# The first block of a two-block model on one core: the norm moved behind the projections, the state-space tables cut in four steps and interleaved with gate projections, memory and load order re-laid

## What is computed

```python
h = rms_norm(x, norm1_g[l])
p = h @ w_in[l]                                  # 1024 -> 512 u, 512 v, 256 s, 2 x 1024 gates
uv = jax.nn.gelu(p[..., :o_s5], approximate=False)
s_in = p[..., o_s5:o_gate]
gates = jax.nn.sigmoid(p[..., o_gate:] + b_gate[l])
br_a = gmlp_spatial_gating(uv[..., :GMLP_WIDTH], uv[..., GMLP_WIDTH:], ...)
br_b = s5_mixer(s_in, ...)                       # two complex linear recurrences, 16 groups of 64 states
merged = g_a * (br_a @ w_up_a[l]) + g_b * (br_b @ w_up_b[l])
x = x + merged @ w_out[l]
h2 = rms_norm(x, norm2_g[l])
x = x + expert_choice_ffn(h2, ...)               # 16 experts of 1024 x 2048 x 1024, 64 tokens each
```

## Time and profile before

| | us |
|---|---|
| median of 3 runs (lowest, highest) | 2056.41 (2055.82, 2056.73) |
| the profiled execution | 2056.92 |
| span of its instructions | 2055.1 |
| TensorE busy in the span | 1782.2 |
| VectorE, ScalarE busy | 675.9, 457.1 |
| start of chunk 19 on TensorE | 410.36 |
| first product of the experts done, ninth load issued | 478 |
| second block starts | about 1381 |

### The profile page before, as it was taken

One profiled execution on the slowest core, in us unless ns is written; L12 is line 12 of the kernel. 1 busy time (PEld: TensorE's weight loads), 2 busy tenths in 40 slices (PEclk: granted clock), 3 DMA queues, 4 the chain that ended last, 5 costly groups with the idle time before them and its releaser, 6 DMA issues. The chain is left out here.

```text
span 2055.1 us, 19088 instructions
## 1 busy us (share of the span) xinstructions
PE 1782.2 (87%) x7952; PEld 1063.1 (52%) x7952; DVE 675.9 (33%) x893; ACT 457.1 (22%) x571; POOL 0.2 (0%) x4
## 2 busy tenths in 40 slices
...
GB/s 140 1 23 136 41 87 72 181 224 272 428 428 428 428 429 428 429 429 429 429 429 429 429 429 428 428 424 166 2 162 43 101 63 102 103 82 110 94 62 41
DMA packets 75428, 492.45 MB, mean 240 GB/s; under 512 B 7024, under 2 KB 11632, under 8 KB 50544
## 3 DMA queue, kind: packets, MB, share of 16 engines
...
## 5 line engine op out<-in xcount | busy, mean ns | idle before, releaser
L670 PE MATMUL ps<-xs,xe 128*64 128x512 f32 x2048 | 461.5, 598 | 66.2 <-DMA xs<-w_up 34.7
L670 PEld LDWEIGHTS ps<-xs,xe 128*64 128x64 f32 x2048 | 141.7, 137 | 378.6 <-issue 264.6
L432 PE MATMUL ps<-xh,hi 128*128 128x512 f32 x576 | 231.8, 402 | 61.3 <-ACT hi L393 60.2
L402 DVE TENSOR_TENSOR lo<-raw,hi 128x2048 fp32r<-128x2048 f32 (+1 forms) x73 | 164.6, 2259 | 321.7 <-ACT hi L393 320.2
L682 PE MATMUL ps<-xs,hidT 128*64 128x512 f32 x1024 | 229.9, 596 | 14.7 <-DMA xs<-w_down 10.0
L432 PE MATMUL ps<-xl,hi 128*128 128x512 f32 x576 | 229.0, 398 | 0.0
L898 DVE TENSOR_TENSOR hid<-hid,ps 128x512 f32<-128x512 f32 x32 | 20.6, 684 | 524.6 <-PE ps L670 524.6
L393 ACT ACTIVATE hi<-raw 128x2048 fp32r<-128x2048 f32 (+1 forms) x73 | 137.5, 1891 | 204.4 <-PE ps L432 125.7
L432 PEld LDWEIGHTS ps<-xh,hi 128*128 128x128 f32 x576 | 111.5, 194 | 89.3 <-issue 61.6
L682 PEld LDWEIGHTS ps<-xs,hidT 128*64 128x64 f32 x1024 | 73.7, 136 | 149.2 <-issue 127.9
L432 PE MATMUL ps<-xh,lo 128*128 128x512 f32 x576 | 136.4, 389 | 0.0
(11 more groups left out here) (417 smaller groups left out, 1782.2 us busy)
## 6 DMA issues: line engine op xcount, KB each, us to landing
...
raw<-w_in SPq DMA_DIRECT2D x25, 1024.0 KB, 10.9
...
```

The source lines that it names most:

```text
L402: dve.tensor_tensor(lo[slot][:, 0:size], raw[:, n % NRAW, 0:size], hi[slot][:, 0:size].bitcast(F32), ALU.subtract).then_inc(sem("lo_done"), 1)
L432: mm = pe.matmul(ps[:, bank + m, 0:nn if token_major else SEQ], l, r, start=(k == 0 and part == 0 and q == 0), stop=(last and part == 1 an ...
L670: mm = pe.matmul(ps[64 * half:64 * half + 64, bank + b, :], xe[:, k, CAP * u:CAP * (u + 1)], xs[n % NXS][:, f:f + 512], start=(k == 0), st ...
```

## The change

The reading, by part:

- **Norm.** `xh` and `xl` are made from x times its gain alone, so chunk 0 needs no norm. The sums of squares move behind chunk 0. The reciprocal root `rb` is applied to the outputs: ACT scales s and v by token (`rtok`) as it empties PSUM, and for u and the gates DVE multiplies PSUM by `rb` into SBUF (`take`); the gelu and sigmoids of ACT then work in SBUF.
- **Order.** The table steps stand between chunks 2, 3, 4, 5 and 6; D after 6; gates a0, b0, a1 come ahead of u; Y and Z follow each other after chunk 10; a projection's second half follows its first at once, and the next waits for PSUM bank by bank (`taken_up_to`).
- **Tables.** `CL` has 9 instead of 17 lags and is kept for all groups, so the 16 copies `CO` go. The products with it write 32 rows each at four places of PSUM (`tables`); Y and Z write 64 rows at two.
- **Memory and loads.** The first block's ring has two slots; chunk n is loaded when chunk n-2 has been split. `INT` is filled by 32 copies instead of 8. Expert chunks 4, 5 and 1 are loaded before chunks 14 and 15.

```diff
-    for h in range(2):
-        first += group(w["w_in"], 1280 + 512 * h, 8) + group(w["w_in"], 2304 + 512 * h, 8)
+    first = group(w["w_in"], 1024, 8, 256) + group(w["w_in"], 512, 8)
+    for c in (1280, 2304, 1792, 0, 2816):
+        first += group(w["w_in"], c, 8)
...
-            if n >= NRAW:
+            if n >= NEXP + NRAW:
                 sp.wait_ge(sem("lo_done"), num(n, i, 1, 1 - NRAW))
-            sp.dma_start(raw[:, n % NRAW, 0:nk * nn].rearrange("p (k n) -> p k n", k=nk), src) \
-                .then_inc(sem(f"raw_in{n % NRAW}"), 16)
+            elif 2 <= n < NFIRST:
+                sp.wait_ge(sem("lo_done"), n - 1)
+            sp.dma_start(raw[:, raw_slot(n), 0:nk * nn].rearrange("p (k n) -> p k n", k=nk), src) \
+                .then_inc(sem(f"raw_in{raw_slot(n)}"), 16)
...
+            pe.wait_ge(sem("qq_taken"), first + 1)
+            return {(0, m): lambda m=m: pe.wait_ge(sem("qq_taken"), first + m + 2) for m in range(3)}
+
+        def first_pe(pe):
+
+            def tables(q):
+
+                pe.wait_ge(sem("tab_q"), q + 1)
+                pe.wait_ge(sem("s_tok"), NT)
+                if q:
+                    pe.wait_ge(sem("vt_done"), 2 * q)
+                for r in range(2):
+                    for g in range(GQ):
+                        mm = pe.transpose(ps[:, PP + r, g * P:(g + 1) * P],
+                                          V[q % 2][:, r, g].rearrange("p t h -> p (t h)"), ident)
+                mm.then_inc(sem("v_ps"), 1)
+                if q == 1:
+                    pe.wait_ge(sem("u_done"), 2)
+                if q >= 2:
+                    pe.wait_ge(sem("hs_done"), q - 1)
+                bank = PP + 2 + q % 2
+                for n, (c0, c1, side, lag) in enumerate(((0, 8, 1, 1), (8, 15, 0, 0), (7, 8, 0, 8))):
+                    for r in range(2):
+                        for j in range(4):
+                            g = GQ * q + j
+                            mm = pe.matmul(ps[32 * j:32 * j + 32, bank, c0 * SH:c1 * SH],
+                                           BF[side][:, r * SG + g:r * SG + g + 2, :].rearrange("p a h -> p (a h)"),
+                                           CL[:, r, g, lag:lag + c1 - c0, :].rearrange("p t h -> p (t h)"),
+                                           start=(n == 0 and r == 0), stop=(n == 2 and r == 1))
+                mm.then_inc(sem("h_ps"), 1)
...
+            norm_sums(pe, 0, QQ + 3)
+            chunk_mms(pe, 1, QQ, 0, 4, xh, xl, True, closes=False,
+                      after={(0, 2): lambda: pe.wait_ge(sem("nrm_rms"), 1)})
+            pe.wait_ge(sem("rb_done"), 1)
+            for t in range(NT):
+                mm = pe.matmul(ps[:, PP, SW + t:SW + t + 1], rb[:, t * P:(t + 1) * P], ident[:, 0:1], start=True, stop=True)
+            mm.then_inc(sem("rt_ps"), 1)
+            chunk_mms(pe, 2, QQ, 4, 4, xh, xl, True, opens=False)
+            tables(0)
+            chunk_mms(pe, 3, QQ, 0, 4, xh, xl, closes=False, after=taken_up_to(pe, 0))
+
...
+            tables(1)
+            chunk_mms(pe, 4, QQ, 4, 4, xh, xl, opens=False)
+            tables(2)
+            chunk_mms(pe, 5, QQ, 0, 4, xh, xl, closes=False, after=taken_up_to(pe, 4))
+            tables(3)
+            chunk_mms(pe, 6, QQ, 4, 4, xh, xl, opens=False)
+
...
+
+            chunk_mms(pe, 7, QQ, 0, 4, xh, xl, closes=False, after=taken_up_to(pe, 8))
+            chunk_mms(pe, 8, QQ, 4, 4, xh, xl, opens=False)
+            chunk_mms(pe, 9, QQ, 0, 4, xh, xl, closes=False, after=taken_up_to(pe, 12))
+            chunk_mms(pe, 10, QQ, 4, 4, xh, xl, opens=False)
+
+            pe.wait_ge(sem("ds_done"), 8)
+            pe.wait_ge(sem("sn_done"), 4)
+            pe.wait_ge(sem("int_in"), 16 * 4 * BL)
+            for g in range(SG // 2):
+                for c in range(2):
+                    o, gg = ps[64 * c:64 * c + 64, PP + g // 4, (g % 4) * P:(g % 4 + 1) * P], g + 8 * c
+                    pe.matmul(o, U[:, gg, :], INT[:, gg, :], start=True, stop=False)
+                    for r in range(2):
+                        mm = pe.matmul(o, Sn[:, r, gg, :], CL[:, r, gg, 0:8, :].rearrange("p t h -> p (t h)"),
+                                       start=False, stop=(r == 1))
+                if g % 4 == 3:
+                    mm.then_inc(sem("y_ps"), 1)
+
...
+            pe.wait_ge(sem("yblk_done"), 2)
+            for q in range(4):
+                for t in range(NT):
+                    for c in range(2):
+                        mm = pe.matmul(ps[64 * c:64 * c + 64, PP + q, t * P:(t + 1) * P],
+                                       vg[:, t, q * P + 64 * c:q * P + 64 * c + 64], wsT[:, 2 * q + c, :],
+                                       start=True, stop=True)
+                mm.then_inc(sem("z_ps"), 1)
+            chunk_mms(pe, 11, QQ, 0, 4, xh, xl, closes=False, after=taken_up_to(pe, 16))
...
+
+            pe.wait_ge(sem("sg_done"), 2)
+            pe.wait_ge(sem("ba_done"), 4)
+            chunk_mms(pe, 13, PP, 0, 4, bah, bal)
+            pe.wait_ge(sem("bb_done"), 2)
+            chunk_mms(pe, 14, QQ, 0, 2, bbh, bbl, after=taken_up_to(pe, 20))
+            pe.wait_ge(sem("mrg_a"), 4)
+            chunk_mms(pe, 15, PP, 0, 4, bah, bal)
+            pe.wait_ge(sem("mrg_b"), 4)
+            chunk_mms(pe, 16, QQ, 0, 2, bbh, bbl)
+            pe.wait_ge(sem("mrg_a"), 8)
+            pe.wait_ge(sem("mh_done"), 4)
+            chunk_mms(pe, 17, PP, 0, 4, xh, xl, closes=False)
+            chunk_mms(pe, 18, PP, 4, 4, xh, xl, opens=False, by_tile=("mh_done", 5))
+            pe.wait_ge(sem("mrg_b"), 8)
+
...
+            for k in range(KD):
+                act.wait_ge(sem(f"x_in{k // 2}"), 16)
+                a(xh[:, k, :], xin[:, k, :], ACT.Copy, scale=gains[:, 0, k:k + 1]).then_inc(sem("xh_done"), 1)
+            make_hi(act, 0)
...
+            def gate(dst, half, second, name, first):
+
+                for m in range(4):
+                    act.wait_ge(sem("qq_taken"), first + m + 1)
+                    c = P_BG + 8 * second + 4 * half + m
+                    a(dst[:, m, :], dst[:, m, :], ACT.Sigmoid, bias=prm[:, c:c + 1]).then_inc(sem(name), 1)
+
+            gate(ga[0], 0, 0, "ga_done", 4)
+            take_tables(2)
+            make_hi(act, 6)
+            act.wait_ge(sem("var_done"), 1)
+            a(sm[:, 128:132], sm[:, 141:149:2], ACT.Sqrt, bias=eps).then_inc(sem("std_done"), 1)
+            make_hi(act, 7)
+            take_tables(3)
+            gate(gb[0], 0, 1, "gb_done", 8)
+            make_hi(act, 8)
...
+
+                gs = slice(GQ * q, GQ * q + GQ)
+                tm = [TMP[:, r].rearrange("p (g t h) -> p g t h", g=GQ, t=9) for r in range(2)]
+                ct = CT[:].rearrange("p r (g h) -> p r g h", g=SG)
+                cmul([CL[:, r, gs] for r in range(2)],
+                     [PT[:, r, gs].unsqueeze(3).to_broadcast([P, GQ, 9, SH]) for r in range(2)],
+                     [ct[:, r, gs].unsqueeze(2).to_broadcast([P, GQ, 9, SH]) for r in range(2)], tm, minus=True)
+                dve.sem_inc(sem("tab_q"), 1)
...
+            def take(dst, n):
+
+                dve.wait_ge(sem("pe_used"), n)
+                for m in range(4):
+                    tt(dst[:, m, :], ps[:, QQ + m, :], rb[:], ALU.mult).then_inc(sem("qq_taken"), 1)
+
+            inputs(0)
+            dve.wait_ge(sem("nrm_rms"), 1)
+            L(dve.reciprocal(rb[:], rb[:]))
+            dve.sem_inc(sem("rb_done"), 1)
+            make_lo(dve, 2)
+            outputs(0)
+            inputs(1)
+            outputs(1)
+            make_lo(dve, 3)
+            inputs(2)
+            outputs(2)
+            make_lo(dve, 4)
+            for t in range(NT):
+                dve.wait_ge(sem("qq_taken"), t + 1)
+                L(dve.bn_stats(sm[:, 96 + 6 * t:102 + 6 * t], vg[:, t, :]))
+                L(dve.bn_aggr(sm[:, 140 + 2 * t:142 + 2 * t], sm[:, 96 + 6 * t:102 + 6 * t]))
+            dve.sem_inc(sem("var_done"), 1)
...
+            inputs(3)
+            outputs(3)
+            make_lo(dve, 5)
+            take(ga[0], 5)
...
+            dve.wait_ge(sem("v_ps"), 4)
+            dve.tensor_copy(WT[:, 0, :, 0], y(28))
+            L(dve.tensor_copy(WT[:, 1, :, 0], y(29)))
...
+            make_lo(dve, 6)
+
...
+            L(tt(HS[:, :, 7 * SH:8 * SH], HS[:, :, 7 * SH:8 * SH], tm, ALU.add))
+            dve.sem_inc(sem("hs_ready"), 1)
+            dve.memset(RD[:, :, 0:1], 0.0)
+            L(dve.tensor_copy(RD[:, :, 1:NB], y(9).unsqueeze(2).to_broadcast([P, SG, NB - 1])))
+            take(gb[0], 7)
+            make_lo(dve, 8)
+
...
+            make_lo(dve, 14)
+            take(gb[1], 13)
+            make_lo(dve, 15)
+            make_lo(dve, 16)
+            for h in range(2):
+                dve.wait_ge(sem("pe_used"), 14 + 2 * h)
+                dve.wait_ge(sem("ga_done"), 4 + 4 * h)
+                for m in range(4):
...
+            d(prm[:], w["small"]).then_inc(sem("cst_in"), 16)
```

(56 more changed lines are left out.)

872 lines of the change are left out of this document (373 added, 499 removed).

## The result

| | us |
|---|---|
| predicted (range) | 1929 (1916 to 1954) |
| measured median of 4 runs (lowest, highest) | 1934.24 (1931.98, 1935.84) |
| before, in the same runs | 2056.57 |
| ratio to before | 0.940 (95% interval 0.939 to 0.942) |
| profiled execution, its span | 1933.9, 1932.1 |

The account below looks back on a forecast made before the run. Expert stage bound by DMA, first block by TensorE waiting for other engines; terms put chunk 19's start at 282.7 against 410.36, 127.7 earlier, so span 1927.4, with 1.8 outside and 0.5 down to the median about 1929 us (1916 to 1954).

Parts of the forecast that it names:

- What bounds: Expert stage bound by DMA, 903 us, can only begin earlier; before chunk 19 TensorE waits 129 us for other engines.
- Start, tables, Y and Z: First block: chunk 0 starts at 20.4 us; four table steps take 8.8; Y takes 7.2 and Z 4.0.
- rival B: Table steps, Y and Z: small tiles do not overlap, or the clock falls at the tables; 1936 to 1944, chance 0.19.
- `lo` 6 and `mrg_a`: TensorE waits 4.4 us in chunk 6 for `lo` 6 behind `WT`, and 4.7 at chunk 15 for `mrg_a`.
- Chunk 9: Its load queues behind 32 `INT` copies, lands at 150, wanted at 158: hidden; only a PSUM bank wait of 0.75 us.
- hidden up to about 0.70: Chunk 9's load stays hidden while each of the 32 `INT` copies takes at most about 0.70 us to issue.
- my own signs of being wrong: Table step of 4 us, chunk 9 waiting, clock 0.5 between chunks, or stage from chunk 19 on not 1645 us.
- waits some 14: At 1.14 us an issue the `INT` copies take 36 us, and chunk 9 waits some 14 us.
- rival C: A queue or splitting engine is late: copies hold chunk 9 by 14 us (1943), VectorE falls back too (1955); chance 0.10.
- The clock: Low-clock spells of 1.66 us behind D and behind chunk 15's wait, 3.4 in all; D itself 12.0 at clock 0.59.
- the row on transposes between chunks: Profile row: eight transposes between dense chunks took 1.0 us at full clock; read as evidence against a clock loss at tables.
- The early loads: Expert chunks 4, 5 and 1 loaded early cost and bring nothing, 0 us, while the DMA idles before the first expert product.

Follow-up runs that it names:

- experiments 3 and 5: Changed kernel with `lo` 6 made ahead of `WT`: 1931.94 us; changed kernel with the first four `mrg_a` passes ahead of `lo` 15 and 16: 1926.35 us.
- experiment 2: Changed kernel with `take` of `ga[1]` ahead of `lo` 9 on VectorE, the load of chunk 9 left late: 1928.75 us.
- experiment 7: Changed kernel with expert chunks 4, 5 and 1 loaded behind the last product of w_out with the others, not early: 1933.86 us.

## Why the prediction was right, and where it was off

- **What bounds.** Right: the expert stage kept its length, and the gain is the start of chunk 19, 124.7 measured against 127.7.
- **Start, tables, Y and Z.** The start and the tables were right within 1 us; rival B's small products without overlap did not come about (2.0 to 2.3 a step). Y and Z overlap better than taken: 5.7 and 3.6 against 7.2 and 4.0, 1.9 less together.
- **`lo` 6 and `mrg_a`.** Right in place and size: 4.6 for 4.4 and 4.9 for 4.7, each with the named cause (experiments 3 and 5).
- **Chunk 9: the term that was mis-sized.** I took 0.45 to 0.6 us for an issue, "hidden up to about 0.70". It was 0.65, inside that bound, and yet the wait was 5.8 instead of 0.75; "if chunk 9 waits" was among my own signs of being wrong. Two numbers of the term were off. The load landed 5.3 us behind its issue instead of the 2.5 of a chunk by bandwidth, 2.8 more. The copies ahead of it are not needed to explain that: in the changed kernel chunk 5, issued at 63.2 with nothing else under way, took as long (KB, us to landing):

```profile
raw<-w_in SPq DMA_DIRECT2D x1, 1024.0 KB, 5.2
```

  And the chunk was wanted at 154.5, not at 158, because the 6.6 us less for D and its spell outweigh the 3.0 more in chunk 6. These two make 6.3. The copies at 0.65 leave 1.2 us of slack against the 158 of the forecast, and 0.75 + 6.3 - 1.2 = 5.85 is the wait. That `take` stands behind `lo` 9 was in the bounds, though not said: 0.70 and "waits some 14" come out only if `hi` 1.9 and `lo` 2.3 are counted behind the landing. What was missed is that this order could be changed (experiment 2). This is rival C in a milder form. An estimate from the figures of the Trainium skill (DMA: Bandwidth & Descriptors, Bandwidth) was 22 to 30 us for the copies. They took 20.8, near its lower end; but those figures are for loads from HBM that GpSimd issues, so this bears them out only loosely.
- **The clock: right in kind, wrong in place.** I put D at 12.0, as it was behind a wait before; it ran at 1.00 in 7.1. But the low clock fell on the products behind the waits, and on three places instead of two: 2.8 in chunk 6, 2.4 in 9 and 10, 1.5 behind chunk 15, 6.7 for 3.4, and 1.5 more in chunk 20, which is the larger part of the 1.8 lost behind chunk 19. That the clock column shows the low level between chunks (0.58 from 119.35 to 125.67) was another of my signs of being wrong.
- **The transposes.** I wrote that the row on transposes between chunks speaks only for four at a time. It is eight, in two groups of four with no gap between them, as many as in a table step; so it bore on rival B more than I let it.
- **The sum.** Chunk 9 with its clock +7.5, chunk 6 with its clock +3.0, the start and chunk 0 +1.1, the stretch behind chunk 19 +1.8; D and the spell behind it -6.6, Y and Z -1.9, the tables -0.4, the rest +0.2: +4.7, which is the span's 1932.1 against 1927.4. That it came out so near is in part luck: errors of 13.6 one way and 8.9 the other cancel.
- **The early loads.** Right: 0 (experiment 7).

What stays open: the parts that were looked at one at a time are worth 7.1 (interleaving), about 8 (halved `CL`, an estimate from the run with its passes doubled) and 7.7 (norm). They need not add up, and together they are 23 of 122. The rest lies by the profile in chunk loads that no longer queue behind the tables, in `V` and `CL` made ahead under chunks 1 and 2, and in the low clock that went with the waits; no run takes these back one by one.
